# Query and key projections of differential attention as seven-product units in a two-layer transformer kernel

## The reference

```python
u = modulate(rmsnorm(h, g_mix[l]), sh2, sc2)
proj = u @ w_in[l]                    # [256, 1024] @ [1024, 7 * 1024]
qa, ka, va, xm, o_pre, ga, gb = jnp.split(proj, split_idx, axis=-1)
ya = diff_attention(qa.reshape(B, S, 8, 2, 64), ka.reshape(B, S, 8, 2, 64), va.reshape(B, S, 8, 128), lam, ...)
yb = mlstm_branch(xm, o_pre, conv_w[l], ...)
merged = jax.nn.sigmoid(ga) * (ya @ w_proj_a[l]) + jax.nn.sigmoid(gb) * (yb @ w_proj_b[l])
h = h + gt2[:, None, :] * (merged @ w_out[l])

def diff_attention(q, k, v, lam, g_subln, lambda_init):
    q, k = rope(q), rope(k)           # halves of 32 features are exchanged, times sin, plus t * cos
    # per block of 128 queries: softmax(q k^T / 8 + mask), for the two components of each of 8 heads
    a = p[:, 0] - lam * p[:, 1]
    o = a @ v                         # then rmsnorm per head
```

## Time and profile before

| | us |
|---|---|
| median of 3 runs | 1180.81 (1180.71 to 1181.24) |
| the profiled execution | 1179.22 |
| its span, from the first to the last instruction | 1177.4 |
| PE busy (matmul records) | 1164.3 |
| DVE busy | 737.2 |
| ACT busy | 352.1 |
| POOL busy | 86.2 |
| mean granted clock of PE, share of full speed | 0.997 |

### The profile page before, as it was taken

One profiled execution on the slowest core, in us unless ns is written; L12 is line 12 of the kernel. 1 busy time (PEld: TensorE's weight loads), 2 busy tenths in 40 slices (PEclk: granted clock), 3 DMA queues, 4 the chain that ended last, 5 costly groups with the idle time before them and its releaser, 6 DMA issues.

```text
span 1177.4 us, 21319 instructions
## 1 busy us (share of the span) xinstructions
PE 1164.3 (99%) x8862; PEld 1076.8 (91%) x8862; DVE 737.2 (63%) x1658; ACT 352.1 (30%) x996; POOL 86.2 (7%) x104
## 2 busy tenths in 40 slices
PE   9999999999999999999999999999999999999997
PEld 7889999998878999999999999988888998888887
DVE  4558888675148866982898888567845231167632
ACT  2111210232124555212321210245333431056542
POOL 0000000200011000022000000310004010001111
PEclk9999999999999999999999999999999999999999
DMA  9969949762655457676599759574524643642311
GB/s 344 366 217 321 315 154 313 290 245 90 219 180 187 150 214 259 236 264 231 185 342 304 235 201 294 193 260 171 146 61 144 215 144 114 187 136 73 117 63 36
DMA packets 164272, 241.78 MB, mean 205 GB/s; under 512 B 14033, under 2 KB 112559, under 8 KB 164176
## 3 DMA queue, kind: packets, MB, share of 16 engines
q1 hardware_dynamic: 156256, 230.45, 57.9%
q10 hardware_dynamic: 6784, 5.74, 1.7%
q0 software_dynamic: 1136, 4.22, 1.1%
HBM read 236.82 MB, written 4.62 MB: 205 GB/s over the span
## 4 chain that ended last, share of the span: by engine, by line
PE 91%; DVE 5%; DMA 2%; ACT 1%; issue 1%; POOL 0%; DVEq 0%; ACTq 0%
PE ps L189 89%; PE ps L192 2%; DVE arena L198 2%; DMA slots<-in_w_proj_a 1%; DVE x L198 1%; DMA slots<-in_w_proj_b 1%; ACT U L195 1%; DVE slots L207 1%; ACT tmps L195 0%; DVE arena L204 0%; DVE rstd L216 0%; DVE tmps L204 0%; DVE slots L198 0%; DVE tmps L198 0%; POOL arena L198 0%
## 5 line engine op out<-in xcount | busy, mean ns | idle before, releaser
L189 PE MATMUL ps<-U,slots 128*128 128x128 f32 (+2 forms) x2800 | 478.7, 330 | 0.0
L189 PEld LDWEIGHTS ps<-U,slots 128*128 128x128 f32 (+1 forms) x2800 | 419.7, 190 | 40.7 <-issue 4.7
L189 PE MATMUL ps<-arena,slots 128*128 128x128 f32 (+1 forms) x1776 | 237.6, 294 | 0.0
L189 PEld LDWEIGHTS ps<-arena,slots 128*128 128x128 f32 x1776 | 225.3, 192 | 8.6 <-issue 0.4
L195 ACT ACTIVATE tmps<-ps 128x256 f32<-128x256 f32 (+2 forms) x151 | 57.4, 383 | 343.4 <-PE ps L189 319.4
L207 DVE CUSTOM_DVE_ANT_0 arena<-arena,tmpA 128x1024 f32<-128x1024 f32 x96 | 118.2, 1275 | 19.3 <-DMA arena<-in_w_adaT 19.1
L195 ACT ACTIVATE arena<-ps 128x256 f32<-128x256 f32 (+3 forms) x150 | 59.5, 416 | 155.9 <-PE ps L189 152.1
L189 PE MATMUL ps<-arena 128*128 128x128 f32 (+7 forms) x940 | 101.9, 287 | 0.9 <-DVE arena L198 0.9
L189 PEld LDWEIGHTS ps<-arena 128*128 128x128 f32 (+2 forms) x940 | 92.4, 181 | 9.8 <-issue 4.2
L189 PE MATMUL ps<-ABT,arena 128*128 128x128 f32 (+5 forms) x752 | 81.9, 271 | 0.0
L189 PEld LDWEIGHTS ps<-ABT,arena 128*128 128x128 f32 (+3 forms) x752 | 72.5, 174 | 0.8 <-issue 0.8
(11 more groups left out here) (199 smaller groups left out, 1140.6 us busy)
## 6 DMA issues: line engine op xcount, KB each, us to landing
slots<-in_w_in SPq DMA_DIRECT2D x14, 2048.0 KB, 10.3
slots<-in_w_down SPq DMA_DIRECT2D x16, 1408.0 KB, 9.8
slots<-in_w_gate SPq DMA_DIRECT2D x18, 1024.0 KB, 8.0
slots<-in_w_up SPq DMA_DIRECT2D x18, 1024.0 KB, 10.8
arena<-in_w_adaT SPq DMA_DIRECT2D x36, 512.0 KB, 6.1
arena<-in_ada_w1T SPq DMA_DIRECT2D x24, 512.0 KB, 7.5
slots<-in_a_in_w SPq DMA_DIRECT2D x6, 2048.0 KB, 9.8
slots<-in_b_in_w SPq DMA_DIRECT2D x12, 1024.0 KB, 5.4
```

What stands on the lines that cost most here:

```text
L189: return Nothing() if self.e is None else self.e.matmul(*a, **k)
```

## The change

`("qk", 0)` to `("qk", 3)` are added to `U7` behind `("va", 1)`. One such unit makes q and k of one pair together, 512 output features. Its weights are fetched as one 2 MB piece of two parts of 256 columns. The steps keep their numbers: the unit of pair p takes steps 8 + 2p and 9 + 2p, as the two `t_linear` did. `s_raw` goes. The unit is built up in a ring of two (`RAW`), and `s_turned` for q and k, eight transfers, stands in the even step behind the unit, behind the first copy of the next unit. `v_rotate` for q and k stands together in the next odd step.

Around it, other jobs change their places. The exponential of an even head moves from the end of step h + 12 to step h + 13, behind `s_u7_mid`. In step 12 `v_da_scores` stands ahead of `v_ml_rows`. In even steps from 14 on `v_da_weights` stands ahead of `v_da_scores`. The modulation passes of steps 14 to 17 go, steps 24, 25, 26 and 30 have two, step 27 and those from 31 have none, and the last four stand in the residual of `w_out`. `v_t7_3` of the units (`pa`, 0) and (`pb`, 0) stands behind `v_s7`. The fetches of groups 13 to 17 come behind the two weight pieces that they were ahead of. `t_ml_turn` takes banks of `S3` instead of `L`, and a small mLSTM copy takes another temporary.

```diff
-            for b in range(2):
-                fetch("q", b)
-                fetch("k", b)
+            for p in range(4):
+                fetch("qk", p)
             for n, g in (("ga", 13), ("gb", 14), ("op", 15), ("pa", 16), ("pb", 17)):
-                fetch("ada", g)
                 fetch(n, 0)
                 fetch(n, 1)
+                fetch("ada", g)
...
-        U7 = [("xm", 1), ("va", 0), ("va", 1)] + [(n, b) for n in ("ga", "gb", "op", "pa", "pb") for b in range(2)]
+        U7 = [("xm", 1), ("va", 0), ("va", 1)] + [("qk", p) for p in range(4)] + [(n, b) for n in ("ga", "gb", "op", "pa", "pb") for b in range(2)]
...
+        RAW = [arena[:, 19368:20392], tmps[:, 3:5, :].rearrange("p i n -> p (i n)")]
...
+            if n == "qk" and b >= 2:
+                return raw_read(b - 2)
+            if (n, b) == ("ga", 0):
+                return raw_read(2)
...
+        def raw_read(pair):
+            return [s_turn[RB.index(n, pair)].at(n, pair) for n in ("q", "k")] + [pool.at("k", "cos", pair)]
...
-            e.wait_ge(*act.at(n, "raw", pair))
-            tb, sig = TC.buf(n, "raw", pair), s_turn[RB.index(n, pair)]
+            done7(e, "qk", pair)
+            tb, sig = raw(n, pair), s_turn[RB.index(n, pair)]
...
# tensor
-                if 8 <= j < 16:
-                    t_linear(e, ("q", "k")[j % 2], (j - 8) // 2, U, u_in("n2"), amid={(1, 0): t_ml_gates_sum} if j == 11 else None)
-                elif j >= 2:
-                    i = (j - 2) // 2 if j < 8 else (j - 10) // 2
-                    (t_u7_second if j % 2 else t_u7_first)(e, i)
+                if j >= 2:
+                    if j % 2:
+                        t_u7_second(e, (j - 2) // 2, t_ml_gates_sum if j == 11 else None)
+                    else:
+                        t_u7_first(e, (j - 2) // 2)
...
# vector
+        PIECES = {18: (0, 1), 19: (1, 2), 20: (2, 3), 21: (3, 4), 22: (4, 5), 23: (5, 6), 24: (6, 8), 25: (8, 10), 26: (10, 12),
+                  28: (12, 13), 29: (13, 14), 30: (14, 16)}
...
-                if j == 12:
-                    v_ml_rows(e)
                 if j == 14:
                     v_ml_source(e)
-                if 13 <= j < 19:
+                if 14 <= j < 19 and j % 2 == 0:
                     v_da_weights(e, j - 13)
                 if 12 <= j < 20:
                     v_da_scores(e, j - 12)
-                if 19 <= j < 21:
+                if j == 12:
+                    v_ml_rows(e)
+                if 13 <= j < 19 and j % 2 or 19 <= j < 21:
                     v_da_weights(e, j - 13)
-                if 10 <= j < 18:
-                    v_rotate(e, ("q", "k")[j % 2], (j - 10) // 2)
+                if 11 <= j < 18 and j % 2:
+                    v_rotate(e, "q", (j - 11) // 2)
+                    v_rotate(e, "k", (j - 11) // 2)
...
                 v_residual(e, "wo", pair, sm[:, 128:136], "n2", 0 if pair >= 2 else None)
+                if pair < 2:
+                    v_ada_blocks(e, 13, 32 + 4 * pair, 36 + 4 * pair)
...
# scalar
-                if 9 <= j < 17:
-                    s_raw(e, ("q", "k")[(j - 9) % 2], (j - 9) // 2)
...
+                if j >= 4 and j % 2 == 0:
+                    s_u7_out(e, (j - 4) // 2)
+                elif j >= 3:
+                    s_u7_mid(e, (j - 2) // 2)
+                    if 13 <= j < 20:
+                        s_da_exp(e, j - 13)
...
-                if 9 <= j < 17:
-                    s_turned(e, ("q", "k")[(j - 9) % 2], (j - 9) // 2)
+                if 10 <= j < 18 and j % 2 == 0:
+                    s_turned(e, "q", (j - 10) // 2)
+                    s_turned(e, "k", (j - 10) // 2)
...
-                if 12 <= j < 20:
+                if 12 <= j < 20 and j % 2:
                     s_da_exp(e, j - 12)
```

More of the change, by code:

```diff
@@ L1585, in done7, with raw @@
             e.wait_ge(*dve.at("7", "c22", *u))
-        def s_raw(e, n, pair):
-            tb, free = TC.open(n, "raw", pair)
-            for f in free:
-                e.wait_ge(*f)
-            e.wait_ge(*pe.at(n, pair))
-            e.activation(tb, L.buf(n, pair), ACT.Copy).then_inc(*act.up(n, "raw", pair))
-            L.close([act.now()], n, pair)
+        def raw(n, pair):
+            return RAW[pair % 2][:, 512 * ("q", "k").index(n):][:, 0:512]
+        def raw_read(pair):
+            return [s_turn[RB.index(n, pair)].at(n, pair) for n in ("q", "k")] + [pool.at("k", "cos", pair)]
         def s_turned(e, n, pair):
@@ L1886, in s_ml_turn @@
             e.wait_ge(*pe.at("mvt", h))
-            e.activation(MVT[:, 2 * h:2 * h + 2, :], two(L.buf("mvt", h)), ACT.Copy).then_inc(*act.up("mvt", h))
-            L.close([act.now()], "mvt", h)
+            e.activation(MVT[:, 2 * h:2 * h + 2, :], two(S3.buf("mvt", h)), ACT.Copy).then_inc(*act.up("mvt", h))
+            S3.close([act.now()], "mvt", h)
         def t_ml_gates(e):
@@ L1906, in s_ml_gates @@
         def s_ml_gates(e):
-            tb, free = TC.open("ml part")
-            for f in free:
-                e.wait_ge(*f)
+            for c in (5, 6, 7):
+                for f in TB.free.get(("xc", c), []):
+                    e.wait_ge(*f)
             e.wait_ge(*pe.at("ml part"))
-            e.activation(tb[:, 0:T], X2.buf("ml part")[:, 0:T], ACT.Copy).then_inc(*act.up("ml part"))
+            e.activation(tmpB[:, 2, 0:T], X2.buf("ml part")[:, 0:T], ACT.Copy).then_inc(*act.up("ml part"))
             X2.close([act.now()], "ml part")
@@ L1923, in t_ml_gates_sum @@
             i.then_inc(*pe.up("ml gates"))
-            TC.close([pe.now()], "ml part")
         def v_ml_gates(e):
@@ L3251, in tensor @@
                         e.wait_ge(*x)
[L3252 removed]
+            for i in (15, 16):
                 t_u7_first(e, i)
```

71 lines of the change are left out of this document (38 added, 33 removed).

## The result

The changed kernel takes 1182.88 us (median of 20 runs, 1180.89 to 1183.94), the kernel before, run beside it, 1180.93 us. The ratio is 1.0016, with a 95% interval of 1.0010 to 1.0021: slower by about 1.9 us, where 3.1 us less was forecast. The ratios in this document are of the means of the fast executions (one of the kernel before took 1986.33 us and is not among them), so they can differ a little from the quotient of two medians. The profiled execution took 1182.18 us, with a span of 1180.4 us against 1177.4.

A forecast was written before the change was run, and what follows sets the result against it. PE was taken to bound the kernel (91% of the chain of waits). -6.5 + 1.2 + 2.2 + 0.5 + 0.9 - 1.4 = -3.1 us gave 1176.1 us profiled, 1177.7 as median, range 1173.8 to 1180.6.

The forecast's parts named there:

- PE's work: Mixing stage: four units of 50.0 us replace eight `t_linear` of 56.5 us, so PE's work falls by 6.5 us.
- ACT's transfers in step 13: Eight transfer issues, 5.0 us, stand ahead of ACT's copies after p6 and p5, so PE waits +1.2 us (0 to 2).
- The exponential of head 0: Step 13: behind ACT's copies it delays DVE's weights and rotations, so PE waits +2.2 us (0 to 3) before head 2's scores.
- Small ones: Steps 13 to 18: copy after p7 behind an exponential, rotation of pair 3 just in time, +0.5 us (0 to 1.2).
- Step 19: DVE, now without slack, lengthens PE's existing wait of 0.81 us by +0.9 us (0 to 1.7).
- Later steps: PE's waits for DVE at p6 of (`pa`, 0) and (`pb`, 0) shrink: -1.4 us (0 to -1.76).
- The four passes in the residual of `w_out`: Four modulation passes, 4.7 us, each two in a 5 us gap, were to cost nothing.
- DVE becomes the bound: Rival: all DVE collisions count and second passes of steps 24 to 26 undo later gains; 1179.7 us, chance 0.20.
- ACT's queue is held: Rival: all 32 issues take 0.92 us, up to four groups show on PE, +8 us, 1185.7 us; chance 0.05.
- The weight loads set the pace: Rival: 0.142 us a record of 128 columns, units 7 us more than the eight `t_linear`, 1188 us; chance 0.01.
- The slower outcome: Sign of the whole change: slower by over 0.2% was given 0.05, faster 0.62, the same 0.33.
- ACT starts nothing: Claim on ACT's transfers in step 13: while they are issued, at 0.63 us or at worst 0.92 each, ACT starts nothing.

The follow-up runs named there:

- e9: e3 with the exchanged copies of q and k made by four transfers of 32 x 1024 instead of eight of 32 x 512: 1177.73 us, ratio 0.9973 to the kernel before.
- e5: e3 with DVE rotating q and k of pair 1 ahead of the weights of head 0 in step 13: 1176.83 us, ratio 0.9963 to the kernel before.
- e11: e10 with the modulation passes of steps 18 and 19 moved into steps 22 and 23: 1182.72 us, ratio 1.0019 to the kernel before.
- e1: Changed kernel with POOL's token squares ahead of the load of the second c row: 1180.38 us, ratio 0.9994 to the kernel before.
- e8: Kernel before with only the last four modulation passes moved into the residual of `w_out` and group 17 fetched later: 1183.68 us, ratio 1.0025.
- e2: Changed kernel with ring `L` advanced one place, restoring the earlier bank assignment: 1180.05 us, ratio 1.0003 to the kernel before.
- e4: Kernel before with ring `L` advanced two places after the mLSTM's transpositions, giving the changed kernel's banks: 1183.65 us, ratio 1.0025.
- e12: Kernel before with ring `L` advanced two places behind the gates of the feed-forward stage: 1182.40 us, ratio 1.0007.
- e3: Changed kernel with both repairs, squares ahead of the c row's load and ring `L` advanced one place: 1179.24 us, ratio 0.9985 to the kernel before.
- e10: e9 with the rotations of pair 1 ahead of the weights of head 0 in step 13: 1176.03 us, ratio 0.9962 to the kernel before.
- e6: e3 with ACT's eight transfers parted, q's four in the even step, k's four in the odd: 1178.00 us, ratio 0.9983 to the kernel before.

## Why the prediction was wrong, point by point

**PE's work: sign right, size off by 1.35.** From 307.19 to 375.97 the kernel before takes 68.78 us, from 308.81 to 375.62 the changed one takes 66.81. With the waits of 3.18 taken off, PE's work fell by 5.15 us, not 6.5 (5.2 was given as the least). The four units took 51.2 us of PE, not 50.0. The product pair takes 3.57 us as read from the earlier trace rows where it follows another pair, but 3.68 where it follows a group of small matmuls (340.17 to 343.85), and the scores and transpositions break each unit in several places. I had counted the switches in the eight `t_linear` and none in the units.

**ACT's transfers in step 13: right in mechanism, in size partly by luck.** 1.17 us for 1.2, in the experiments up to 1.72. The group of eight took 5.6 us (343.51 to 349.13), not 5.0, as one issue took 1.23; the other three groups took 5.0 to 5.2, 0.63 to 0.65 an issue. PE, less its late start, wanted the copy 0.8 us later than I had laid out (348.45 less 1.62 is 346.83, for 346.05), which hid that. e9 shows that it is the number of issues.

**The exponential of head 0: right in size, half right in cause.** 2.01 us for 2.2. DVE was idle 2.14 us for it. But e9 shows that 1.6 us of wait stay when it comes earlier, as DVE's own queue is nearly as late. What removes them is the order on DVE (e5).

**Small ones: 0.28 for 0.5**, at the scores of head 6 (1.21 us for 0.93).

**Step 19: 0.33 for 0.9, and not by DVE alone.** The wait is 1.14 against 0.81. DVE has lost its slack, as forecast:

```profile
403.41 0.29 DVE L207 CUSTOM_DVE_ANT_0 arena<-ps,cst 128x128 f32<-128x128 f32 x1
```

It starts on the scores of head 7 1.24 us behind PE's start of them, before 0.95 us (403.19 less 402.24). But I had ACT nowhere in that step, and ACT is as late: e11 gives DVE its slack back, and the wait stays at 1.14.

**Later steps: 1.23 for 1.4.** The stalls of the earlier trace rows went, 1.76 us, and 0.66 came at 467.86 us.

Up to the end of the units the sum is 2.60 for the forecast 3.1 us. It is so near in part by luck: PE's work brought 1.35 us less, and the waits of steps 13 to 19 together cost 1.0 us less than forecast (3.8 for 4.8).

**The four passes in the residual of `w_out`: "nothing". This step failed first of all**, by 2.3 us (from -2.60 to -0.34 in the account). I had priced the passes on DVE and the slot that they hold, and both were right. I had not asked who waits for what comes after them: `v_ada_mods(17)` moved too, POOL's program stands on it, and behind that wait stand the squares. The wait is in the code of `gpsimd`, and the earlier trace rows had made me look at POOL for its clashes with DVE only. e1 takes it away, e8 makes it alone.

**The ring of banks: no step at all.** I told that `t_ml_turn` takes banks of `S3` in place of `L` and gave it no consequence. Ahead of the second block's scores `L` has handed out four tiles fewer, and a wait of 1.47 us appeared 650 us behind the change (e2, e4, e12). This is the second term that was put at nothing. With both repaired (e3, 1179.24 us) the kernel lies inside the forecast's range.

**The rivals.** "DVE becomes the bound" (1179.7) holds in step 19 only together with ACT, and in step 13 once the transfers are fewer. "ACT's queue is held" needed groups of over 6 us; they took 5.0 to 5.6 in the changed kernel's profile and 6.2 once in e3's. Its +8 us was no sum: four groups at 2.3 us each would be 9.2. "The weight loads set the pace" did not come. The slower outcome came from none of the rivals that I had priced.

**What stays open.** In the medians the change loses 1.9 us, in the account of the two profiles 1.3. The clock's falls, below, and single slow issues of ACT (one took 1.23 us in the changed kernel's step 12) come and go between executions, and I did not separate them in the runs that have no profile.

## What to carry to other kernels

When a step moves, list every program that waits for its signal and what is queued behind that wait, on the idle engines too: an engine at 7% still orders its work. When tiles leave or join a ring that the whole program shares, compare at every later hand-over which tile had the bank before and after; a skipped place costs no instruction and puts it right. And where a queue of issues stands ahead of a copy that PE needs, fewer and larger transfers help, while parting them only moves the wait.

## What the runs showed of the hardware

**PE's clock can fall behind a wait of 1.45 to 2.1 us.** Windows of e1, behind its wait of 2.00 us at 357.9 us. Columns: PE, PEld, DVE, ACT and POOL busy (records), granted clock, DMA share and rate:

```profile
356.00:359.50 3.50, 1.57 (x15) 1.25 (x16) 3.43 (x5) 0.45 (x2) 0.00 (x0) 1.00 0.74 242
359.50:363.00 3.50, 3.50 (x21) 3.50 (x20) 3.43 (x7) 0.38 (x1) 0.50 (x1) 0.56 0.88 358
```

The 32 records from 359.13 take 5.47 us, not 3.84. It happened in six of the twelve profiles of experiments (e1, e3, e8, e9, e10, e11), each time right behind a wait of 1.45 to 2.1 us, and not in e2, e6 or the changed kernel, which have waits of 2.0 us too, nor behind the wait of 1.45 us in step 14 of e11. It costs up to 1.6 us, less where PE would have waited soon after, as in e3, where the wait ahead of the scores of head 2 shrank to 0.58. What decides it stays open. So a wait of 2 us costs 2 us in one execution and 3.6 in another, and the forecast had only the first.

**An issue of a transfer holds back what stands behind it in ACT's program, here for about 0.61 us.** The median of the 32 issues of the exchanges is 0.61 us (0.51 to 1.23), and eight take 5.0 to 5.6 us. What stands ahead of them in the program still runs beside them: the last operation on `rows` starts at 344.78 us, among the issues of 343.51 to 349.13. So "ACT starts nothing" in the prediction holds for what comes behind. e9 shows an issue of twice the bytes at the same 0.6 us. Bytes alone do not set the length: other issues of ACT in this kernel take 0.30 to 0.55 us, and that of a 2 MB transfer 0.39. The Trainium skill, "DMA: Bandwidth & Descriptors", section "Issuing engines are not separate DMA queues", says that the sequencer's time to start a DMA "is usually small relative to the DMA itself". Here it is not: one of these transfers of 64 KB lands 2.6 or 4.7 us behind its issue (the medians of the two buffers), no later than the group of eight takes to issue, and the issues are on the path.
